# Opening, token order and last FFN set of a hybrid attention, gMLP and SwiGLU layer on 8 cores

## The reference

```
mod   = silu(c) @ w_ada + b_ada                      # six vectors of 1024: shift, scale, gate, twice
h     = LN(x) * (1 + scale) + shift                  # same for the context tokens, with c_ctx
q, k, v, u, vb, ga, gb = split(h @ w_in)             # 512, 128, 128, 512, 512, 1024, 1024
ya    = attention(rope(q), rope(k), v)               # window of +-128 tokens, all context keys, a sink
yb    = gelu(u) * (W_s LN(gelu(vb)) + b)             # per chunk of 128 tokens and group
x_mid = LN(alpha * x + gate1 * ((sigmoid(ga) * (ya @ w_a) + sigmoid(gb) * (yb @ w_b)) @ w_out))
h2    = LN(x_mid) * (1 + scale2) + shift2
out   = LN(alpha * x_mid + gate2 * ((silu(h2 @ w_gate) * (h2 @ w_up)) @ w_ffn_out))
```

## Time and profile before

| quantity | value |
|---|---|
| median of 3 runs | 982.81 us (980.55 to 983.01) |
| profiled execution: span, slowest core | 977.1 us (cores 970.7 to 977.1) |
| its time beyond the span | no time of its own is given; the median is 5.7 us above its span |
| PE / DVE / ACT / POOL busy | 892.7 / 501.3 / 340.0 / 455.5 us |
| mean granted TensorE clock, by core | 0.977 to 0.985 |

### The profile page before, as it was taken

The page is one execution under the profiler, slowest core; times in us unless marked ns, Lnnn a source line. Parts: engine busy times, 40 slices in busy tenths (PEclk is TensorE's granted clock), DMA queues, the critical chain, the costliest instruction groups (busy, mean ns, idle before and its releaser), DMA issues.

```text
span 977.1 us, 15797 instructions; the slowest of 8 cores (970.7 to 977.1 us)
## 1 busy us (share of the span) xinstructions
PE 892.7 (91%) x5357; PEld 425.8 (44%) x5357; DVE 501.3 (51%) x999; ACT 340.0 (35%) x520; POOL 455.5 (47%) x436
## 2 busy tenths in 40 slices
PE   1467999989999999999799999999999999999991
PEld 1324644544555444444344444444444444444440
DVE  3345645677767325664445564332368333332287
ACT  0225565766565122455332443111144111101132
POOL 7337764232222556977754476231186431422034
PEclk9979999999999999999899999999999999999995
DMA  9999764046563698464465145653446763534013
GB/s 194 176 227 208 185 96 66 7 67 103 87 104 55 158 188 172 98 119 85 130 128 118 52 134 142 135 112 76 73 139 177 161 141 86 120 75 87 1 43 129
DMA packets 52223, 113.76 MB, mean 116 GB/s; under 512 B 4656, under 2 KB 5936, under 8 KB 52144
## 3 DMA queue, kind: packets, MB, share of 16 engines
q0 software_dynamic: 27664, 54.47, 34.8%
q1 hardware_dynamic: 24480, 58.29, 19.6%
HBM read 156.71 MB, written 8.39 MB: 169 GB/s over the span
## 4 chain that ended last, share of the span: by engine, by line
PE 78%; DMA 11%; issue 4%; POOL 3%; DVE 2%; ACT 1%; SPq 0%; DVEq 0%; POOLq 0%; ACTq 0%
PE psum L563 72%; DMA arena<-wvb 4%; DMA arena<-wada 3%; PE psum L732 2%; PE psum L766 2%; DMA arena<-xh 1%; DMA arena<-wout 1%; DMA arena<-wff 1%; POOL arena L817 1%; PE psum L843 1%; ACT arena L736 1%; PE psum L647 1%; POOL arena L555 1%; PE psum L748 0%; POOL arena L865 0%
## 5 line engine op out<-in xcount | busy, mean ns | idle before, releaser
L563 PE MATMUL psum<-arena 128*128 128x512 bf16 (+2 forms) x3792 | 816.7, 373 | 21.7 <-DVE arena L674 8.0
L563 PEld LDWEIGHTS psum<-arena 128*128 128x128 bf16 x3792 | 359.1, 98 | 443.3 <-issue 52.9
L865 POOL TENSOR_TENSOR arena<-arena 128x512 bf16<-128x512 f32 x88 | 113.0, 1290 | 133.4 <-DMA arena<-wff 82.4
L883 ACT ACTIVATE arena<-psum 128x512 f32<-128x512 f32 x88 | 52.4, 595 | 290.4 <-PE psum L563 288.1
L884 DVE TENSOR_TENSOR arena<-psum,arena 128x512 bf16<-128x512 f32 x88 | 60.8, 691 | 166.6 <-PE psum L563 159.4
L575 DVE BATCH_NORM_STATS2 arena<-arena 128x6 f32<-128x512 f32 x120 | 81.0, 688 | 54.4 <-ACT arena L712 24.9
L736 ACT ACTIVATE arena<-psum 128x1024 bf16<-128x1024 f32 x80 | 79.7, 1024 | 33.5 <-PE psum L732 33.3
L898 DVE TENSOR_TENSOR arena<-psum,arena 128x1024 f32<-128x1024 f32 x48 | 58.8, 1225 | 48.2 <-PE psum L563 43.7
L808 DVE SCALAR_TENSOR_TENSOR arena<-arena,psum 128x512 f32<-128x512 f32 x64 | 43.6, 683 | 58.6 <-PE psum L563 58.2
L804 ACT ACTIVATE arena<-psum 128x512 f32<-128x512 f32 x64 | 38.1, 598 | 88.9 <-PE psum L563 88.0
L811 POOL TENSOR_TENSOR arena<-arena 128x512 bf16<-128x512 f32 x32 | 41.2, 1288 | 49.8 <-DVE arena L808 49.6
(11 more groups left out here) (89 smaller groups left out, 650.6 us busy)
## 6 DMA issues: line engine op xcount, KB each, us to landing
arena<-wff SPq DMA_DIRECT2D x88, 256.0 KB, 3.3
arena<-wff POOLq DMA_DIRECT2D x22, 1024.0 KB, 11.1
arena<-xh SPq DMA_DIRECT2D x30, 512.0 KB, 7.1
arena<-wada POOLq DMA_DIRECT2D x24, 512.0 KB, 10.0
arena<-wc POOLq DMA_DIRECT2D x16, 768.0 KB, 8.1
out<-arena SPq DMA_DIRECT2D x15, 512.0 KB, 3.0
arena<-wout SPq DMA_DIRECT2D x8, 512.0 KB, 5.5
arena<-xh POOLq DMA_DIRECT2D x4, 512.0 KB, 34.2
```

The source lines that it names most:

```text
L563: r = e.matmul(out, lhsT=pairs[i][0], rhs=pairs[i][1], start=(i == 0), stop=(i == n - 1))
L865: G.op('pool', lambda e, fi=fi, hs=hs, stg=stg: e.tensor_tensor(out=w2[i % 5][:, fi, hs], in0=stg, in1=g2bc[:, hs], op=ALU.mult))
L883: G.op('act', lambda e: e.activation(out=sg, in_=ps[0], func=AF.Silu))
```

## The change

- Token order: the host puts the 2048 own tokens first and the two halo tiles last (16, 17); attention, the slices of `hT` and the rope tables follow.
- Opening: x tiles 0 to 3 go first on SP; POOL's queue is held to a given order: w_ada 0, ident, w_ada 1 to 5, w_u 0 and 1, w_ada 6 and 7, w_u 2 and 3, w_qk 4, perm, x 4, x 5, w_qk 0, x 6, w_qk 1, x 7, w_qk 2, w_qk 3, w_v, w_vb. Eight x buffers for tiles 0 to 7, four after, four buffers for normalised tiles.
- `a1` handles four tiles: per chunk four 128x128 matmuls against the identity (ordinary matmuls, fp32 out) fill a bank, and one 128x512 eviction empties it. Halo and context tiles go in twos.
- The norm still adds the negated mean, as before; only a variable's name differs.
- The planner's constants and its DMA model change.
- Order: u before k and q in group 0; w_ada steps move from the projections into attention; the halo's k and v move before attention.
- Last half: sets (0,1), (2,3), (4,5), (6 to 10), with 20 `gu` calls in the set before the last, and four bank pairs in turn in the last.
- `tail` keeps sums and intermediate results in the two PSUM banks; 1/std goes to another 32-byte cell; tile 14's last step is put after tile 15's gamma step.

```diff
-    RATE = 310e3
-    MARGIN = 1.0
-    PEMARGIN = 1.0
-    XMARGIN = 0.4
+    ENGINES = 16.0
+    MARGIN = 2.0
+    PEMARGIN = 0.2
+    XMARGIN = 0.15
...
+    xr = [at(x, F32, D) for x in (78, 82, 86, 90, 102, 106, 131, 135)]
+
+    def xslot(n):
+        return xr[n if n < 8 else n % 4]
+    wada1 = [at(98, BF16, 8, 256), at(88, BF16, 8, 256)]
+    xnb = [at(x, BF16, D) for x in (110, 112, 94, 96)]
...
-    def a1_pair(i, b0, split, after=(), loads=True):
-        which = 0 if tiles[2 * i][0] == 'x' else 1
-        for p in range(2):
...
-            G.op('pool', lambda e, src=src, dst=dst, rstd=rstd, neg=neg: e.tensor_scalar(
-                out=dst, in0=src, scalar1=neg, scalar2=rstd, op0=ALU.add, op1=ALU.mult))
-            for h in range(2):
-                def f(e, h=h, dst=dst, p=p):
-                    pt = bkb(b0 + h).rearrange('p (c t q) -> p c t q', c=4, t=2)
-                    for c in range(4):
-                        r = e.transpose(pt[:, c, p], dst[:, (4 * h + c) * 128:(4 * h + c + 1) * 128], ident)
-                    return r
-                G.op('pe', f, dur=4 * 0.058)
-        ti = tiles[2 * i][1]
...
+    def a1(first, n, banks, split=False):
+
+        kind, ti = tiles[first]
+        which = 0 if kind == 'x' else 1
+        w = 128 * n
+        xs = []
+        for i in range(n):
+            src, dst = xslot(first + i), xnb[nx[0] % 4]
+            nx[0] += 1
+            rstd, mu = stats(src, 1024)
+            G.op('pool', lambda e, src=src, dst=dst, rstd=rstd, mu=mu: e.tensor_scalar(
+                out=dst, in0=src, scalar1=mu, scalar2=rstd, op0=ALU.add, op1=ALU.mult))
+            xs.append(dst)
         for c in range(8):
-            pt = bkb(b0 + c // 4)[:, (c % 4) * 256:(c % 4 + 1) * 256]
-            dst = (hcT if which else hT)[:, c, ti * 128:(ti + 2) * 128]
+            pt = bk(banks())[:, 0:w]
+
+            def f(e, c=c, pt=pt):
+                for i in range(n):
+                    r = e.matmul(pt[:, i * 128:(i + 1) * 128], lhsT=xs[i][:, c * 128:(c + 1) * 128], rhs=ident,
+                                 start=True, stop=True)
+                return r
+            G.op('pe', f, dur=n * 0.058)
+            dst = (hcT if which else hT)[:, c, ti * 128:ti * 128 + w]
             sc_, sh_ = mcol(1, c, which), mcol(0, c, which)
             if c % 2 == 0 or not split:
...
-        srcs = [(kT[:, (j + s) * 128:(j + s + 1) * 128], vaug[:, j + s]) for s in range(3)]
+        where = [j - 1 if j else NT, j, j + 1 if j < NT - 1 else NT + 1]
+        srcs = [(kT[:, p * 128:(p + 1) * 128], vaug[:, p]) for p in where]
...
-        if t >= NT - 1:
+        rs = dens[:, t % 2, 0, 0:1]
+        if t == NT - 1:
...
+                G.op('dve', lambda e, h=h: e.tensor_tensor(out=bk(b0 + h), in0=bk(b0 + h), in1=acc[:, half(h)], op=ALU.add))
+                G.op('dve', lambda e, h=h: e.bn_stats(out=st[:, 6 * h:6 * h + 6], in_=bk(b0 + h)))
...
+            G.op('dve', lambda e: e.tensor_scalar(out=rs, in0=mv[:, 1:2], scalar1=EPS, scalar2=None, op0=ALU.add))
+            G.op('pool', lambda e: e.tensor_tensor(out=rs, in0=rs, in1=neghalf[:, 0:1], op=ALU.pow))
...
+                    out=bk(b0 + h), in0=bk(b0 + h), scalar=mv[:, 0:1], in1=ln2g[:, half(h)], op0=ALU.subtract,
                     op1=ALU.mult))
+            held[0]()
...
-                    out=acc[:, half(h)], in0=y[:, half(h)], scalar=mv[:, 3:4], in1=ln2b[:, half(h)], op0=ALU.mult,
+                    out=acc[:, half(h)], in0=bk(b0 + h), scalar=rs, in1=ln2b[:, half(h)], op0=ALU.mult,
...
-                out=acc[:, half(h)], in0=bk(b0 + h), scalar=1.0, in1=acc[:, half(h)], op0=ALU.mult, op1=ALU.add,
+                out=bk(b0 + h), in0=bk(b0 + h), scalar=1.0, in1=acc[:, half(h)], op0=ALU.mult, op1=ALU.add,
                 accum_out=st[:, h:h + 1]))
...
+        G.op('act', lambda e: e.activation(out=junk, in_=bk(b0, 2), func=AF.Square, bias=mv[:, 0:1], scale=1.0,
                                            accum_out=st[:, 8:9]))
-        G.op('dve', lambda e: e.scalar_tensor_tensor(out=y, in0=acc, scalar=mv[:, 0:1], in1=ln2g, op0=ALU.add,
+        yy = bk(b0, 2) if t == NT - 2 else y
+        G.op('dve', lambda e: e.scalar_tensor_tensor(out=yy, in0=bk(b0, 2), scalar=mv[:, 0:1], in1=ln2g, op0=ALU.add,
...
+        G.op('dve', lambda e: e.tensor_scalar(out=rs, in0=st[:, 8:9], scalar1=1.0 / D, scalar2=EPS, op0=ALU.mult,
                                               op1=ALU.add))
...
+        G.op('pool', lambda e: e.tensor_tensor(out=rs, in0=rs, in1=neghalf[:, 0:1], op=ALU.pow))
+
+        def close():
+            if t == NT - 2:
+                G.op('dve', lambda e: e.scalar_tensor_tensor(out=acc, in0=yy, scalar=rs, in1=ln2b, op0=ALU.mult,
+                                                             op1=ALU.add))
+            else:
+                G.op('act', lambda e: e.activation(out=acc, in_=y, func=AF.Copy, scale=rs))
+                G.op('pool', lambda e: e.tensor_tensor(out=acc, in0=acc, in1=ln2b, op=ALU.add))
+            G.finals.append(load(out_d[t * 128:(t + 1) * 128, :], acc))
+        if t == NT - 2:
+            held.append(close)
         else:
-            G.op('dve', lambda e: e.scalar_tensor_tensor(out=acc, in0=y, scalar=mv[:, 3:4], in1=ln2b, op0=ALU.mult,
-                                                         op1=ALU.add))
-        G.finals.append(load(out_d[t * 128:(t + 1) * 128, :], acc))
+            close()
...
+    for n in range(4):
+        x_load(n)
...
-    cast_load(ident, ident_d)
-    cast_load(perm, perm_d)
...
-    for i, h in enumerate((0, 4, 1, 5, 2, 6, 3, 7)):
-        wl = cast_load(flat(wada0[i]), wada_d[h])
-        col_block(h, wada0[i], i % 2)
...
-        lq = cast_load(flat(wqk[:, m]), wqk_d[m])
-    for m in range(4):
-        lu = cast_load(flat(wu[:, m]), wu_d[m])
...
+    first_load(0)
+    cast_load(ident, ident_d, queued=True)
+    for i in range(1, 6):
+        first_load(i)
+    cast_load(flat(wu[:, 0]), wu_d[0], queued=True)
+    cast_load(flat(wu[:, 1]), wu_d[1], queued=True)
+    first_load(6)
+    l0 = first_load(7)
+    cast_load(flat(wu[:, 2]), wu_d[2], queued=True)
+    cast_load(flat(wu[:, 3]), wu_d[3], queued=True)
+    cast_load(flat(wqk[:, 4]), wqk_d[4], queued=True)
+    cast_load(perm, perm_d, queued=True)
...
-    a1_pair(0, 2, True)
-    a1_pair(1, 4, True)
-    a1_pair(2, 6, True)
-    rope_load(0, 640, [lq])
-    lx = [x_load(n) for n in range(6, 10)]
-    rope_load(640, 1152, [lu])
-    lw = cast_load(flat(wv), wv_d, order=lx)
-    lv = cast_load(flat(wvb), wvb_d, order=[lw])
-    cast_load(flat(masks), masks_d, order=[lv])
-    lw = cast_load(flat(wst), wst_d, order=[lv])
-    load(esink, esink_d, after=[lv])
-    load(glgc, glgc_d, after=[lv])
...
+        col_block(first[i], wada0[i], i % 2)
+    a1(0, 4, Banks(2, 3, 4, 5, 6, 7), True)
+    rope_load(0, 512, [l0])
+    x_load(4)
+    x_load(5)
+    cast_load(flat(wqk[:, 0]), wqk_d[0], queued=True)
+    x_load(6)
+    lq = cast_load(flat(wqk[:, 1]), wqk_d[1], queued=True)
+    x_load(7)
+    cast_load(flat(wqk[:, 2]), wqk_d[2], queued=True)
+    lx = cast_load(flat(wqk[:, 3]), wqk_d[3], queued=True)
+    lw = cast_load(flat(wv), wv_d, queued=True)
+    lv = cast_load(flat(wvb), wvb_d, queued=True)
+    rope_load(512, 1024, [lq])
+    for n in range(8, 12):
+        x_load(n, after=[lx])
...
-    ada_i = [0]
+    ada_i, ada_n = [0], [0]
+
+    def ada_slot(i):
+        return (wada1 if i < 8 else wada1b)[i % 2]
+
+    def ada_load():
+        i = ada_n[0]
+        ada_n[0] += 1
+        if i < 16:
+            cast_load(flat(ada_slot(i)), wada_d[ada[i]], order=[lw])
 
...
-        w = (wada1 if i < 8 else wada1b)[i % 2]
-        cast_load(flat(w), wada_d[ada[i]], after=[lw])
-        (bc_block if ada[i] // 4 in (2, 5) else col_block)(ada[i], w, bank)
+        if i < 16:
+            (bc_block if ada[i] // 4 in (2, 5) else col_block)(ada[i], ada_slot(i), bank)
+            ada_load()
...
-    for g in range(4):
-        if g == 0:
-            a1_pair(3, 6, False, loads=False)
-        elif g < 3:
-            a1_pair(2 * g + 2, 6, False, after=[lv], loads=g > 1)
-            if g == 1:
-                rope_load(1152, 1664, [lv])
...
-                a1_pair(9, 6, False, after=[lw])
-        else:
-            a1_pair(8, 6, False)
-        if g < 2:
-            k_unit(g, A2B)
-            for m in range(4):
-                q_unit(m, g, A2B)
...
         for m in range(4):
-            u_unit(m, g, A2B)
-            if g:
-                if m < 3 and ada_i[0] < 8:
-                    ada_step(A2B())
-        for t in range(4 * g, 4 * g + 4):
-            vb_unit(t, A2B)
-            if g < 2:
-                v_unit(t, A2B)
-        if g == 1:
-            kc_unit(A2B)
-            v_unit(18, A2B)
-            v_unit(19, A2B)
-            G.op('dve', lambda e: e.tensor_copy(out=scb, in_=sc[:, 0:8].unsqueeze(2).to_broadcast([128, 8, 128])))
...
+        u_unit(m, 0, A2B)
+    k_unit(0, A2B)
```

(55 more changed lines are left out.)

143 lines of the change are left out of this document (84 added, 59 removed).

## The result

The changed kernel takes 950.9 us (median of 4 runs, 949.6 to 952.5) against 982.9 us: 0.9682 of the time before, 95% interval 0.9637 to 0.9726 (the two medians alone would give 0.9674). Run twice more on other chips it came to 0.9688 (0.9667 to 0.9708) and 0.9669 (0.965 to 0.9689). The sign was right, the size was not.

A forecast was written before the change was run, and what follows sets the result against it. PE bounds the kernel, with 84 us idle plus time at a lower clock to win; the opening is bound by DMA arrivals. 977.1 - 11.5 - 9 = 956.6 us span, plus 5.7 gives 962.3 us; range 953 to 973.

The forecast's parts named there:

- the one that gave the planner nothing: Whole kernel: the sum of gains had no term for the planner's new constants and DMA model, so 0 us.
- rival A: 44 to 500 us: thin planner margins make PE wait on early handoffs; slower than before, say 988 us; chance 0.05.
- Rival D: 125 to 500 us: the new order also removes half of 12 us of PE idle time; 956 us; chance 0.08.
- Term one: The end: PE, not the DVE, sets the pace of the last tiles and the tail shortens; -11.5 us.
- the lock between POOL and the DVE: The end: reading one operand from PSUM stops POOL stretching the DVE's gamma step, 3.32 us down to 1.25.
- Rival C: The end: square sum and gamma step run in sequence, so the DVE still sets the pace; 5 us, 967; chance 0.12.
- The 3.8 us "for the store": The tail: time from the DVE's last step to the span's end, kept at 3.8 us as before.
- Term two: The opening: waits behind the rope product and a late x tile go; -9 us.
- counts for nothing alone: The opening: one 128x512 eviction (0.60 us) for two of 128x256 (1.15) relieves ACT but gains no time.
- The 7.5 us behind the rope product: The opening: PE's single 7.5 us wait goes, as the rope pair is issued at 43, not 50 us.
- Rival B: The opening gives nothing: same bytes before 77 us, DMA full, x 4 to 7 late; 971.3 us; chance 0.17.
- The 5.7 us between the span and the median: Whole kernel: the profiled span lies 5.7 us below the runs' median, kept and added to the forecast span.

The follow-up runs named there:

- e1: Kernel before with only the changed end (tail, sets, gu distribution, bank pairs): 0.9865 of the kernel before.
- e9: Kernel before with the changed kernel's end and planner, its opening as before: 0.9778 of the kernel before, 958.9 us.
- e3: Changed kernel, its order made with the planner of before (margins, DMA model, cost of a DMA issue): 0.9749 of the kernel before.
- e10: Changed kernel with the planner's three margins of before (1.0, 1.0, 0.4) and the new DMA model: 0.9769 of the kernel before.
- e6: Changed kernel with its norm in PSUM, but half B's last set of three rounds again: 0.9726 of the kernel before, 957.2 us.
- e2: Changed kernel with the end of the kernel before, opening and planner kept: 0.9754 of the kernel before.
- e5: Changed kernel, five rounds kept, with sums, square sum and gamma step of tiles 0 to 14 in SBUF again: 0.9652 of the kernel before.
- e13: Repeat of the changed kernel with tiles 0 to 14's norm in SBUF, beside the changed kernel on one chip: 0.9648 of the kernel before, 950.2 us.
- e8: Changed kernel with token tiles transposed two to a bank, not four: 0.9731 of the kernel before, 956.9 us.
- e4: Changed kernel with its 160 tile transposes again in transpose mode with bf16 results: 0.9715 of the kernel before, 956.1 us.

## Why the prediction was wrong

**The step that failed** is the one that gave the planner nothing. "The planner's allowance for a handoff to PE falls" stood as rival A only, with a loss; the new DMA model is in no term; and the forecast left "the remaining idle time" after 85 us "as it is". The planner is worth 14.5 us alone, 8.5 us once the end is in (e1 to e9) and 6 to 8 us in the changed kernel (e3). The rival's mechanism (thin margins make PE wait) had the wrong sign as a whole: with the old margins (e10) PE is idle for 3 us more from 85 to 500 us.

The forecast fits the changed kernel with the old planner: 956.6 us of span were forecast, and e3's slowest core takes 957.1 (in the means of the cores 21.8 us less than before, against 20.5 forecast). Of the 11.4 us that were missed, then, 6.1 are the planner (spans of e3 and the changed kernel, means of the cores), 4.0 the base (below), and some 1 is left.

By kind of time, in the means of the cores, the 27.9 us by which the spans fell are: 9.1 us less idle time of PE until 125 us, 2.1 from 125 to 500, 3.5 in the last set, 7.9 of tail, and 5.3 us less busy time of PE. The last is the clock, 0.987 to 0.988 after and 0.980 before over all executions; the prediction had 1 to 2 us for it. Rival D, that half of the waits between 125 and 500 us go too, came nearer with its time (956), but these waits shrank by 2.1 us, not 6.

**Term one, the end, -11.5 us.** The size was right: 11.7 us in the traces of e1, 13.3 us in the times, and in the changed kernel PE's gap of 4.0 us and 7.0 us of the slowest cores' tails. The tail was put at 11.1 us and is 11.5, by two misses that cancel: from PE's end to the DVE's end 6.6 us, not 7.3, and from there to the end of the span 5.0, not 3.8. The reasons were half right. Five rounds are what counts: taking them back costs 4 to 6 us (e6) of the 7 that the whole end is worth with the new planner (e2). But with that planner PE does not wait in the last set in any version, three rounds or five, so what they give there is a shorter tail (the DVE's last step starts 11.3 us after PE's end in e6, 5.2 us in the changed kernel), and not the pace. How e1's 13.3 us divide under the old planner was not run. That the lock between POOL and the DVE had to go is wrong. The gamma step takes 1.28 us in all 15 tiles with PSUM and up to 4.0 us without, but with five rounds this costs PE nothing, and e5 and e13, which keep the lock, are no slower. By the Trainium skill's rule (SBUF — State Buffer, "Who interferes with whom") two SBUF inputs lock and one does not; by that rule, the traces agree. Rival C was right in mechanism (square sum and gamma step one behind the other, 11.8 against 9.8 us of tail) and too dear: PE lost nothing. The 3.8 us "for the store" behind the DVE's last step hold a wait of that store for the one before it (1.4 us); it grew to 2.6.

**Term two, the opening, -9 us.** With the old planner it gives 11.4 us (0.9865 to 0.9749), with the new one 9 us (e9). The last block came when forecast, 42.5 (42.59), w_qk 0 and 1 some 4 us later than their 54 and 57 (57.7 and 61.4 as used), and the idle time between 44 and 88 us was less than 8 (6.0 until 85). The closeness of the 9 us is partly luck, since the sum has a slip: 44 us, 35.2 of work, 8 of waits and 2 to 3 of clock end at 89 to 90, not 88, which leaves 7 to 8. The eviction's 0.60 us was read from a plain copy; with scale and bias it takes 0.78. That the wide eviction "counts for nothing alone" was wrong: four tiles to a bank are worth 4.5 us in the trace, 4 to 6 in the times (e8), only in part by the banks. The 7.5 us behind the rope product went because the pair is issued 8 us sooner; u ahead of k and q was not needed. Rival B (nothing) is ruled out by e9 against the changed kernel.

**The base.** The 5.7 us between the span and the median were kept as a constant. The runs list the spans of all cores: the time lies 1.6 to 2.2 us above the slowest core's span in the kernel before, 1.5 to 1.6 in the changed one. The profiled execution of the kernel before was a short one (mean of its cores 974.2 us, 976.6 in the mean of 46 executions), and in the changed kernel the cores also differ less (slowest above mean: 3.3 us, 4.9 before). By spans alone the change is 27.9 us, by times 31 to 32; 4.0 us of the miss are this (5.7 us kept, 1.7 found).

What stays open: which single waits the pair of margins and model removes, whether other orders would do as well, why the clock is higher with the new planner, and what e4's 3 to 5 us are.

The version with the norm in SBUF (e5, e13) is the best that was run, 949.9 and 950.2 us, 0.965 of before.

## What to carry to other kernels

Where a list scheduler writes the order, its constants are part of the kernel: a change of them moves every engine's order and can be worth more than the code that is changed with it, so price them by a run and not by zero, and do not expect the parts to add up. Make the final set deep enough that the engine that normalises has caught up when PE ends, and look for the tail's length in what can still run side by side after PE's last matmul, and in what the last store waits for; a lock between two engines costs only what the pace does not cover. Take several executions' spans as the base of a sum, not one execution's distance to a median.
